# Second attention: the third group of turned weights goes into the free half of a score bank, ahead of the scores, and VectorE copies it out

## The reference, cut to what matters

```python
def diff_attend(q, k, v, lam):
    s = jnp.einsum('bqhmd,bkhmd->bhmqk', q, k, preferred_element_type=jnp.float32)
    a = jax.nn.softmax(s * (1.0 / math.sqrt(ATTN_HEAD_DIM)), axis=-1)
    a = a[:, :, 0] - lam * a[:, :, 1]
    return jnp.einsum('bhqk,bkhe->bqhe', a.astype(v.dtype), v)

def head_out(o, subln_g, lam_init):
    b, t = o.shape[:2]
    return (rmsnorm_2(o, subln_g) * (1.0 - lam_init)).reshape(b, t, ATTN_V_W)
```

## Time and profile before

| | |
|---|---|
| median of 3 runs | 2702.0 us (2698.88 to 2703.53) |
| time of the profiled execution | 2697.34 us |
| its span | 2696.1 us |
| PE busy in the span | 2597.3 us (96%) |
| DVE busy | 1830.7 us (68%) |
| ACT busy | 1303.7 us (48%) |
| POOL busy | 511.9 us (19%) |
| the attention of this change | about 1738 to 1968 us of the span |

### The profile page before, as it was taken

How to read it: one execution, slowest core, us unless ns; L and a number is a source line. 1 busy time by engine, 2 the same in 40 slices (tenths; PEclk the granted TensorE clock), 3 DMA queues, 4 the chain that set the end, 5 groups by cost and what they waited for, 6 DMA issues and landing times. The chain is left out here.

```text
span 2696.1 us, 35795 instructions
## 1 busy us (share of the span) xinstructions
PE 2597.3 (96%) x13421; PEld 2200.0 (82%) x13421; DVE 1830.7 (68%) x2193; ACT 1303.7 (48%) x2014; POOL 511.9 (19%) x729
## 2 busy tenths in 40 slices
PE   8999999999999999999999999989997699999996
PEld 7799997888898787778888898878876588888885
DVE  4288887633458888875557433489845788888887
ACT  4255553511343333333445221188723477777775
POOL 5722220000022222221101310022233100000102
PEclk9999999999999999999999999999998899999998
DMA  8700101111323445657655422001234699999998
GB/s 304 263 25 25 32 13 40 48 47 47 118 99 112 149 152 172 194 177 283 211 190 170 115 60 73 5 21 33 70 144 194 233 383 396 396 395 393 396 395 276
DMA packets 249515, 461.90 MB, mean 171 GB/s; under 512 B 16588, under 2 KB 138176, under 8 KB 247936
## 3 DMA queue, kind: packets, MB, share of 16 engines
q1 hardware_dynamic: 218944, 352.73, 37.2%
q0 software_dynamic: 30288, 106.84, 12.1%
q10 hardware_dynamic: 112, 0.03, 0.0%
HBM read 384.79 MB, written 65.32 MB: 167 GB/s over the span
## 5 line engine op out<-in xcount | busy, mean ns | idle before, releaser
L508 PE MATMUL ps<-r,r 128*128 128x512 f32 (+4 forms) x10508 | 2302.2, 377 | 11.9 <-DVE r L493 4.0
L508 PEld LDWEIGHTS ps<-r,r 128*128 128x128 f32 (+1 forms) x10508 | 1879.1, 188 | 364.2 <-issue 10.5
L485 ACT ACTIVATE r<-f 128x2048 fp32r<-128x2048 f32 (+2 forms) x339 | 503.8, 1495 | 386.0 <-PE ps L508 383.1
L3739 DVE TENSOR_TENSOR r<-f,r 128x2048 fp32r<-128x2048 f32 x188 | 429.1, 2291 | 63.9 <-ACT r L485 62.5
L493 DVE TENSOR_TENSOR r<-f,r 128x1024 fp32r<-128x1024 f32 (+1 forms) x151 | 167.8, 1125 | 322.3 <-ACT r L485 322.3
L508 PE MATMUL ps<-f,f 128*128 128x128 f32 (+1 forms) x1218 | 152.2, 275 | 2.9 <-ACT f L1288 2.3
L508 PEld LDWEIGHTS ps<-f,f 128*128 128x128 f32 x1218 | 143.8, 192 | 5.9 <-issue 4.5
L876 DVE SCALAR_TENSOR_TENSOR f<-f,misc,f 128x1023 f32<-128x1023 f32 (+29 forms) x120 | 146.4, 1259 | 0.0
L2018 ACT ACTIVATE r<-f 128x512 fp32r<-128x512 f32 x140 | 87.0, 629 | 72.7 <-PE ps L508 57.6
L3757 POOL DMA_INDIRECT ff_scratch<-f,misc x15 | 29.0, 1936 | 474.2 <-ACT f L3868 442.5
L2025 DVE TENSOR_TENSOR r<-f,r 128x512 fp32r<-128x512 f32 x140 | 106.2, 762 | 7.6 <-ACT r L2018 7.6
(11 more groups left out here) (349 smaller groups left out, 2279.3 us busy)
## 6 DMA issues: line engine op xcount, KB each, us to landing
f<-in_w_gate_dram SPq DMA_DIRECT2D x64, 1024.0 KB, 9.0
f<-in_w_up_dram SPq DMA_DIRECT2D x64, 1024.0 KB, 10.9
f<-in_w_down_dram SPq DMA_DIRECT2D x64, 1024.0 KB, 8.8
f<-in_w_in_dram SPq DMA_DIRECT2D x56, 512.0 KB, 4.4
f<-in_w_ada_dram SPq DMA_DIRECT2D x96, 256.0 KB, 4.7
f<-in_w_ffn_in_dram SPq DMA_DIRECT2D x80, 256.0 KB, 4.1
hid_scratch<-f POOLq DMA_DIRECT2D x77, 256.0 KB, 2.8
f<-hid_scratch SPq DMA_DIRECT2D x35, 512.0 KB, 5.1
```

Source lines behind the costliest of these rows:

```text
L485: self.act.activation(hi, raw, ACT.Copy).then_inc(self.sem(st.name + "_hi"), 1)
L508: return self.pe.matmul(o, left, right, start=start, stop=stop, skip_group_check=True)
L3739: self.dve.tensor_tensor(es.lo[i % 4], es.raw[i % 8], es.hi[i % 4].bitcast(F32), ALU.subtract).then_inc(self.sem("e_lo"), 1)
```

## The change

Per unit the third group of turns (two squares, 256 columns) no longer uses banks 6 and 7. A new `turn_p_last` puts it into columns 256 to 511 of bank 2 (for the last unit bank 5) and stands ahead of the scores of map 0 in PE's order. DVE copies it to SBUF with a new `copy_p_last`, first in DVE's iteration, in place of ACT. The last piece of the scores of map 0 (two passes) lies in that same bank and now waits for this copy. The inverse of map 0's sum is left out: `copy_v` copies without a scale, and POOL makes up for it by using EPS times the square of that sum in the norm (one small instruction more per unit, and ACT's next-but-one exponentials wait for it). Banks 6 and 7 then have four uses in an iteration.

```diff
@@ turns
-                uses += [("p", u - 2, g, "a2_p", 3 * (u - 2) + g + 1) for g in range(3)]
+                uses += [("p", u - 2, g, "a2_p", 2 * (u - 2) + g + 1) for g in range(2)]
@@ pe_scores2
         for c in range(3):
+            if (mp, c) == (0, 2) and u >= 2:
+                pe.wait_ge(*sem("a2_pd", u - 1))
@@ pe_attention2
+        def turn_p_last(u):
+            pe.wait_ge(*sem("a2_mix", u + 1))
+            if u < n - 1:
+                pe.wait_ge(*sem("a2_exp0", u + 2))
+            else:
+                pe.wait_ge(*sem("a2_exp1", n))
+            o = self.last_turned(u)
+            for c in range(2):
+                t = pe.transpose(o[:, c * P:(c + 1) * P], self.PA[0][u % 3][:, (8 + c) * P:(9 + c) * P], self.ident)
+            t.then_inc(sem("a2_pTd"), 1)
...
         for u in range(n + 3):
+            if 2 <= u <= n + 1:
+                turn_p_last(u - 2)
             if 0 < u < n:
                 self.pe_scores2(u, 0)
@@ last_turned
+        return self.ps[:, 2 if u < len(self.PAIRS) - 1 else 5, 256:512]
@@ act_attention2
-            act.activation(self.OM2[j], ps[:, 6 + k % 2, 0:P], ACT.Copy, scale=self.r8[u % 3][0]).then_inc(
-                sem("a2_val"), 1)
+            act.copy(self.OM2[j], ps[:, 6 + k % 2, 0:P]).then_inc(sem("a2_val"), 1)
@@ dve_attention2
-            if u >= 3:
-                dve.wait_ge(*sem("a2_val", u - 2))
...
-            dve.reciprocal(r_[1], s_[1]).then_inc(sem("a2_fac"), 1)
-            dve.reciprocal(r_[0], s_[0]).then_inc(sem("a2_fac"), 1)
+            dve.reciprocal(r_, s_[1]).then_inc(sem("a2_fac"), 1)
...
+        def copy_p_last(u):
+            dve.wait_ge(*sem("a2_pTd", u + 1))
+            if u >= 2:
+                dve.wait_ge(*sem("a2_pv", u - 1))
+            elif u == 1:
+                dve.wait_ge(*sem("mc_lo", 1))
+            dve.tensor_copy(self.PTb[u % 2].rearrange("p a b -> p (a b)"), self.last_turned(u)).then_inc(sem("a2_pd"), 1)
...
         for u in range(n + 3):
+            if 2 <= u <= n + 1:
+                copy_p_last(u - 2)
             if 0 < u < n:
                 self.dve_largest2(u, 0)
@@ pool_attention2
+            pool.wait_ge(*sem("a2_exp0", u + 1))
+            pool.tensor_scalar(e, s0, s0, EPS, ALU.mult, ALU.mult).then_inc(sem("a2_po"), 1)
+            pool.wait_ge(*sem("a2_po", 3 * u + 1))
             pool.wait_ge(*sem("a2_sq", u + 1))
-            pool.tensor_scalar(ss, ss, 1.0 / P, EPS, ALU.mult, ALU.add).then_inc(sem("a2_po"), 1)
+            pool.tensor_scalar(ss, ss, 1.0 / P, e, ALU.mult, ALU.add).then_inc(sem("a2_po"), 1)
```

More of the change, by code:

```diff
@@ L3124, in pe_attention2 @@
         n = len(self.PAIRS)
+        def turn_p_last(u):
[8 more added lines that the diff above has]
+            t.then_inc(sem("a2_pTd"), 1)
         def turn_p(u):
-            pe.wait_ge(*sem("a2_mix", u + 1))
-            for g in range(3):
+            for g in range(2):
                 k = self.turn_use("p", u, g)
                 self.pe_turn_bank(k)
-                w = (4, 4, 2)[g]
-                for c in range(w):
+                for c in range(4):
                     t = pe.transpose(ps[:, 6 + k % 2, c * P:(c + 1) * P],
@@ L3141, in values @@
             for c in range(10):
-                if c in (0, 4, 8):
-                    pe.wait_ge(*sem("a2_p", 3 * u + c // 4 + 1))
+                if c in (0, 4):
+                    pe.wait_ge(*sem("a2_p", 2 * u + c // 4 + 1))
+                elif c == 8:
+                    pe.wait_ge(*sem("a2_pd", u + 1))
                 v = self.V2[:, c, h * P:(h + 1) * P] if c < 8 else self.V2c[:, c - 8, h * P:(h + 1) * P]
@@ L3190, in expo @@
             elif mp == 0 and u >= 3:
-                act.wait_ge(*sem("a2_pT", 3 * (u - 2)))
+                act.wait_ge(*sem("a2_pT", 2 * (u - 2)))
+                act.wait_ge(*sem("a2_po", 3 * (u - 3) + 1))
             elif mp == 0:
@@ L3198, in copy_p @@
             j = u % 2
-            for g in range(3):
+            for g in range(2):
                 k = self.turn_use("p", u, g)
-                o = self.PTa[j][:, 4 * g:4 * g + 4, :] if g < 2 else self.PTb[j]
-                act.wait_ge(*sem("a2_pT", 3 * u + g + 1))
+                act.wait_ge(*sem("a2_pT", 2 * u + g + 1))
                 if u >= 2:
@@ L3206, in copy_p @@
                     act.wait_ge(*sem("mc_lo", 1))
-                act.copy(o.rearrange("p a b -> p (a b)"), ps[:, 6 + k % 2, 0:(4, 4, 2)[g] * P]).then_inc(
+                act.copy(self.PTa[j][:, 4 * g:4 * g + 4, :].rearrange("p a b -> p (a b)"), ps[:, 6 + k % 2, :]).then_inc(
                     sem("a2_p"), 1)
@@ L3280, in mix @@
             dve.wait_ge(*sem("a2_exp1", u + 1))
-            if u >= 3:
-                dve.wait_ge(*sem("a2_val", u - 2))
             if u == 0:
                 dve.wait_ge(*sem("lm", 5))
-            dve.reciprocal(r_[1], s_[1]).then_inc(sem("a2_fac"), 1)
-            dve.reciprocal(r_[0], s_[0]).then_inc(sem("a2_fac"), 1)
-            dve.wait_ge(*sem("a2_fac", 3 * u + 1))
-            dve.tensor_scalar(r_[1], r_[1], s_[0], self.lamc[:, 5:6], ALU.mult, ALU.mult).then_inc(sem("a2_fac"), 1)
-            dve.wait_ge(*sem("a2_fac", 3 * u + 3))
-            dve.scalar_tensor_tensor(out=self.PA[0][j], in0=self.PA[1][u % 2], scalar=r_[1], in1=self.PA[0][j],
-                                     op0=ALU.mult, op1=ALU.add).then_inc(sem("a2_mix"), 1)
+            dve.reciprocal(r_, s_[1]).then_inc(sem("a2_fac"), 1)
+            dve.wait_ge(*sem("a2_fac", 2 * u + 1))
+            dve.tensor_scalar(r_, r_, s_[0], self.lamc[:, 5:6], ALU.mult, ALU.mult).then_inc(sem("a2_fac"), 1)
+            dve.wait_ge(*sem("a2_fac", 2 * u + 2))
+            dve.scalar_tensor_tensor(out=self.PA[0][j], in0=self.PA[1][u % 2], scalar=r_, in1=self.PA[0][j],
+                                     op0=ALU.mult, op1=ALU.add).then_inc(sem("a2_mix"), 1)
+        def copy_p_last(u):
[5 more added lines that the diff above has]
+            dve.tensor_copy(self.PTb[u % 2].rearrange("p a b -> p (a b)"), self.last_turned(u)).then_inc(sem("a2_pd"), 1)
         def low_o(u):
```

22 lines of the change are left out of this document (11 added, 11 removed).

## The result

The changed kernel takes 2722.6 us (median of 6 runs, 2721.4 to 2725.8) against 2702.8 us (median of 6, 2698.9 to 2706.0): a ratio of 1.0077, 95% interval 1.0066 to 1.0088. It is 20 us slower, where I forecast 11 and a range up to 18. The profiled execution took 2722.43 us (span 2721.2), 25.1 more than the profiled one of before.

The account below looks back on a forecast made before the run. DVE was taken to set the pace where it never idles, POOL to stand in PE's way elsewhere. Terms 10.9 + 2.4 - 2.1 = +11.2 us on the 2702.0 median gave 2713 us, range 2704 to 2720.

Parts of the forecast that it names:

- full intervals: 12 attention-loop intervals without DVE idle before map 0's first reduction; each predicted 0.91 us longer, +10.9 us.
- half full: 7 attention-loop intervals with 0.37 to 0.77 us DVE idle before map 0's first reduction; predicted +2.4 us.
- free, with what is given back: 11 intervals with 1.03 us or more DVE idle: 0; shorter ones behind stretched ones, 0.3 us in about seven places: -2.1.
- The copy and its hand-over: DVE's copy 0.41, hand-over to PE 0.05, short score passes to reduction 0.45, in series: 0.91 us where DVE never idles.
- Only the copy counts: Rival: the score passes mostly don't wait, so only DVE's 0.41 us copy costs: +3 us, 2705; chance 0.14.
- PE's removed waits: PE's waits for ACT's copy and `copy_v` vanish, but DVE covers them or POOL allows only 0.18 us: 0.
- The missing reciprocal: One DVE reciprocal fewer per unit, the factor at best a few hundredths earlier: 0, bound 2.5 us.
- The clock: Named sign of a wrong forecast: the granted clock falls because PE waits more; no size given.

Follow-up runs that it names:

- 12th kernel: The changed kernel with POOL's 128 x 128 multiplication by the norm's factor made by ACT, POOL computing only the factor; 2710.1 us, 1.0028 of the kernel before.

## Why the prediction was wrong

The direction was right and the time was not: 2722.6, above 2713 and above the range. The intervals say which terms held. The middle column is the kernel with the multiplication on ACT:

| term | predicted | without meetings (12th kernel) | after |
|---|---|---|---|
| full intervals | +10.9 | +12.3 | +12.9 |
| half full | +2.4 | +2.5 | +4.4 |
| free, with what is given back | -2.1 | -2.6 | +5.3 |
| sum | +11.2 | +12.2 | +22.5 |

The medians of the runs give 8 us for the twelfth kernel and 20 for the change. Part of the difference is the 2.9 us that the twelfth wins behind the 30 intervals, part is the spread of the profiled executions in other stages (behind those steps, where the kernels are the same, they differ by up to 4.5 us). So the agreement of 11.2 and 12.2 holds for the loop, not for the whole time.

*The copy and its hand-over*: right. 0.41 us, 0.06, and 0.55 for the passes in place of 0.45, in series behind the stack part. Three kernels show it from three sides: moved ahead of the stack part or into bank 5 a full interval costs 0.22 to 0.33 instead of 0.9 to 1.0, doubled it costs 0.46 more. "Only the copy counts" was wrong for bank 2 and describes bank 5.

*PE's removed waits, 0*: right as far as they bring nothing by themselves. They are gone (26.8 us to 2.2) and the time went into the wait for DVE's copy (28.0) and for POOL.

*The missing reciprocal, 0*: right, kept or left out makes no difference (2722.1 and 2722.6; in bank 5 2701.2 both).

*The half full intervals and what is given back*: right in size where no meeting disturbs them (+2.5 and -2.6), and in part by luck. In the twelfth kernel one half full interval, the one that ends at unit 8, grew by 1.75 us where its share of the forecast is 0.54, and the free one behind it shrank by 1.99; in the first of the two the clock stood at 1.2 GHz for a while (below). The other half full ones grew by 0.8 together, not 1.8, and the other free ones gave back 0.6, not 1.8.

*The failing step* is the one on the free intervals. I wrote "DVE gets the turned squares while it idles; it has 1.03 us or more, so 0", and on PE's removed waits "POOL allows 0.18 of it ... I take 0". Both treat POOL's 0.61 us as a fixed length. It isn't. When PE runs ahead and DVE's `mix` starts before POOL's multiplication, that multiplication takes 1.9 us and stands on PE's way. The free intervals cost +5.3 us instead of -2.1. The interval by interval difference between the change and the twelfth kernel is 10.3 us, and seven intervals hold it, those ending at units 10, 17, 19, 25, 27, 29 and 31 (1.56, 3.20, 0.67, 1.57, 1.59, 0.87 and 0.85 us).

*The clock*, which I had named as a danger and not priced: behind the PE wait of 1.96 us in front of 1859.10 the granted clock is 0.50, the 1.2 GHz level, from 1859.8 to 1863.1 us, and the values' weight loads take 3.90 us instead of 2.31. The stretches of the kernel after, in the columns of the first fence (the middle one takes in both levels):

```profile
1855.00:1860.00 5.00, 3.13 (x21) 2.55 (x19) 4.88 (x6) 3.58 (x11) 2.98 (x4) 0.97 0.00 0
1860.00:1865.00 5.00, 5.00 (x28) 4.82 (x28) 0.87 (x3) 2.03 (x5) 0.65 (x2) 0.68 0.02 3
1865.00:1870.00 5.00, 5.00 (x39) 4.57 (x37) 4.93 (x7) 4.02 (x7) 1.06 (x3) 1.00 0.01 2
```

That one place is the 3.20 in the list, about 1.6 us of it the clock's. Behind the long multiplication at 1974.05 it happened once more (3.94 us for the same loads). Behind the other six meetings the clock stayed at 1.00, and the intervals grew only by the wait or less; the kernel with the inverse kept has its seven meetings without one such fall. The clock also stood at 0.50 from 1774.5 to 1777.7 and from 1791.6 to 1794.8 us, behind waits of PE for DVE's copy of 2.51 and 2.17 us. The first lies in a full interval, which grew by 1.02 us like its neighbours. The second lies in the one that ends at unit 8, 7.34 us long; in the kernel with the copy made twice the clock is at 1.00 there, and it is 6.63. So the clock cost up to about 0.7 us there, for which the prediction has no term.

Could it have been read from the kernel before? Partly. Its timelines of DVE and POOL have one meeting that I passed over, since I looked at POOL only in one pair of intervals:

```profile
1796.29 1.55 DVE L3290 SCALAR_TENSOR_TENSOR f<-f,misc,f 128x1280 f32<-128x1280 f32 x1
1796.92 1.40 POOL L3333 TENSOR_SCALAR f<-f,misc 128x128 f32<-128x128 f32 x1
...
1855.41 1.55 DVE L3290 SCALAR_TENSOR_TENSOR f<-f,misc,f 128x1280 f32<-128x1280 f32 x1
...
1899.95 0.61 POOL L3333 TENSOR_SCALAR f<-f,misc 128x128 f32<-128x128 f32 x1
1899.98 1.69 DVE L3290 SCALAR_TENSOR_TENSOR f<-f,misc,f 128x1280 f32<-128x1280 f32 x1
```

It was a multiplication of 1.40 us among its neighbours of 0.61. The margins could be read there too, 0.27 us at 1855 and 0.03 at 1899.95; that the change would use them up could not be read off, only named as a case. A rival "POOL falls behind `mix`", at 1.3 us for every second of some 14 undisturbed intervals, +9, would have widened the range to 2722.

Which of the two moved, `mix` or POOL? The DVE and POOL timelines tell, with times taken from DVE's second reduction of the iteration. The same unit in the kernel before and in the one after (its `mix` and multiplication of 1856.95 and 1857.10 stand above):

```profile
1844.20 1.48 DVE L3269 TENSOR_REDUCE misc<-ps 128x1 f32<-128x1280 f32 x1
1848.86 0.61 POOL L3333 TENSOR_SCALAR f<-f,misc 128x128 f32<-128x128 f32 x1
1848.89 1.68 DVE L3290 SCALAR_TENSOR_TENSOR f<-f,misc,f 128x1280 f32<-128x1280 f32 x1
```

```profile
1852.38 1.48 DVE L3286 TENSOR_REDUCE misc<-ps 128x1 f32<-128x1280 f32 x1
```

Before, POOL multiplies 4.66 us behind the reduction and `mix` starts at 4.69, so the margin was 0.03 us; after, POOL is at 4.72 and `mix` at 4.57. POOL has become 0.06 us later: its chain from the squares to the multiplication is 0.17 longer (1.60 for 1.43), and the squares start 0.1 earlier. `mix` has become 0.12 earlier. In the five units that meet from 1872.87 on the margin before was 0.03 to 0.16 us; POOL is some 0.07 later in all of them and `mix` 0.1 to 0.24 earlier. (The seventh, at 1806.33, had a margin of 1.25 us, behind an interval in which DVE had waited 2.60.) In the kernel with the inverse kept POOL hasn't moved, and `mix` alone makes the seven meetings. So mostly it is `mix` that comes earlier.

What stays open: how much of the 20 us in the medians the meetings take. The loops of the two profiled executions say 10.3, with 1.6 of the clock in it, which another execution need not have.

## What to carry to other kernels

An instruction's length is a measurement in one order of starts: before taking 0 for an engine that is let run ahead, list every length of the short instructions on the way there, and ask of the longest what began just before it. A free half bank is free only for as long as its other half isn't wanted; put the borrowed columns into the bank whose scores come last, and copy them out where the copying engine has something to do in the meantime. And when several engines are nearly full, a wait taken from one of them shows up on the next: price where the freed engine will stand then, before counting the wait as a gain.

## What the runs showed of the hardware

POOL's multiplication of 128 x 128 in SBUF takes 0.61 us, unless DVE is already in a pass that reads two operands from SBUF. The traces of this case hold 414 of these multiplications between 1740 and 2000 us of their spans. 350 are short (under 0.7 us), and not one of them starts inside such a pass; 64 are long (1.19 to 2.71), and 63 of them do (44 in `mix`, 19 in a rest of the output weights), the last one in the same hundredth (1956.05 in the kernel with the inverse's part alone). Each of the 63 ends 0.39 to 0.50 us behind the end of DVE's pass or pair of passes, whatever its lead. In the kernel after: 1856.95 + 1.55 = 1858.50, and 1857.10 + 1.89 = 1858.99. It isn't only `mix`. The DVE and POOL timelines of the kernel before have this row behind the attention's scores:

```profile
1965.61 2.36 DVE L493 TENSOR_TENSOR r<-f,r 128x1024 fp32r<-128x1024 f32 x2 [1.54 <-ACT r L485]
...
1965.65 2.71 POOL L3333 TENSOR_SCALAR f<-f,misc 128x128 f32<-128x128 f32 x1
```

Two rests of the output weights in a row, 0.04 us ahead, hold POOL for both. The size of POOL's own work hardly matters: an instruction on one column took 1.56 us instead of 0.27. DVE's reductions from PSUM hold nothing; 169 of the 350 short multiplications start while one runs. 40 more start inside DVE's copy from PSUM to SBUF. A wide pass with one operand from SBUF and none from PSUM doesn't occur at such a moment, so these traces can't say what it would do.

The Trainium skill (SBUF — State Buffer, SBUF: two separate sides) says that VectorE and GpSimd share a pair of ports as an exclusive lock: a VectorE instruction with two SBUF inputs or a GpSimd one that reads SBUF, whichever starts first, keeps it to its end, and the other is fully blocked. The trace agrees for POOL, in all 63 cases. It doesn't agree the other way round: `mix` started 0.27 us behind POOL's multiplication, with 0.34 us of that still to come, and took its usual 1.55; started 0.03 us behind, where 0.58 was left, it took 1.69. The measurement decides: VectorE loses at most 0.14 us there, and POOL 1.3. By the page alone each order would cost the second engine the rest of the first one's instruction.
